# Second attention with position term and sink by TensorE products, input products in two sweeps, four probability buffers

## What is computed

```python
def second_block(x, p, w_in, w_pool, pool_scale, attn_sinks, w_out, ln1_g, ln1_b, ...):
    z = h @ w_in[i]                       # 1024 -> 512 (u_pool) + 512 (q) + 128 (k) + 128 (v)
    ...
    y_pool = pool_mixer(u_pool, w_pool[i], pool_scale[i])
    y_attn = sliding_window_attention(q, k, v, attn_sinks[i])
    mix = jnp.concatenate([y_pool, y_attn], axis=-1) @ w_out[i]
    h = layer_norm(DEEPNORM_ALPHA * h + mix, ln1_g[i], ln1_b[i])

def sliding_window_attention(q, k, v, sinks):   # 8 query heads, 2 key heads of 64, blocks of 128
    ...
    dist = (qi[:, None] + BLOCK - kj[None, :])
    bias = -slopes[:, :, None, None] * dist.astype(jnp.float32)[None, None]
    scores = jnp.where(mask[None, :, None, None], scores + bias[None, None], NEG_INF)
    m = jnp.maximum(jnp.max(scores, axis=-1, keepdims=True), sink)
    e = jnp.exp(scores - m)
    denom = jnp.sum(e, axis=-1, keepdims=True) + jnp.exp(sink - m)
    probs = (e / denom).astype(v.dtype)
```

## Time and profile before

| what | us |
|---|---|
| median of 3 runs (1540.32 to 1541.84) | 1541.45 |
| the profiled execution's own time | 1541.43 |
| its span in the profile | 1539.7 |
| TensorE busy | 1391.6 |
| VectorE busy | 503.3 |
| ScalarE busy | 310.0 |
| end of the input products to start of the `w_out_2` products | 48.4 |

### The profile page before, as it was taken

The page is one execution under the profiler, slowest core; times in us unless marked ns, Lnnn a source line. Parts: engine busy times, 40 slices in busy tenths (PEclk is TensorE's granted clock), DMA queues, the critical chain, the costliest instruction groups (busy, mean ns, idle before and its releaser), DMA issues.

```text
span 1539.7 us, 17201 instructions
## 1 busy us (share of the span) xinstructions
PE 1391.6 (90%) x6736; PEld 748.1 (49%) x6736; DVE 503.3 (33%) x913; ACT 310.0 (20%) x454; POOL 26.1 (2%) x41
## 2 busy tenths in 40 slices
PE   4998997989899899899899889999998878899998
PEld 2774455434334333334334334334333557699986
DVE  2646434213113113112112111121121454655565
ACT  3415232101101101101001001001011343544451
POOL 1000002000000000000000000000000200000000
PEclk9999997999999999999999999999999877999999
DMA  9208906899999999999999999999999630556540
GB/s 375 117 20 359 421 17 215 359 428 429 429 428 429 429 428 428 429 429 428 429 428 429 429 429 428 429 428 428 428 429 424 223 100 11 200 177 189 190 137 28
DMA packets 62680, 499.98 MB, mean 325 GB/s; under 512 B 6200, under 2 KB 22616, under 8 KB 34928
## 3 DMA queue, kind: packets, MB, share of 16 engines
q1 hardware_dynamic: 59472, 492.85, 77.7%
q0 software_dynamic: 1840, 5.82, 1.2%
q10 hardware_dynamic: 1328, 0.77, 0.2%
HBM read 498.37 MB, written 1.05 MB: 324 GB/s over the span
## 4 chain that ended last, share of the span: by engine, by line
PE 65%; DMA 22%; DVE 8%; issue 3%; ACT 1%; SPq 1%; DVEq 0%; ACTq 0%; PEldq 0%
PE bank L1447 28%; DMA ring<-in_w 20%; PE bank L586 17%; PE bank L624 15%; PE bank L644 2%; DMA ring<-in_w_ada 2%; DVE dk L699 1%; DVE mrows L703 1%; DVE dk L693 1%; PE bank L597 1%; PE bank L632 1%; PE bank L606 1%; DVE w_lo L446 1%; PE bank L1741 0%; PE bank L1629 0%
## 5 line engine op out<-in xcount | busy, mean ns | idle before, releaser
L586 PE MATMUL bank<-ring,xn 128*64 128x512 f32 x2048 | 468.0, 611 | 65.7 <-DMA ring<-in_w 64.1
L586 PEld LDWEIGHTS bank<-ring,xn 128*64 128x64 f32 x2048 | 163.5, 140 | 359.9 <-issue 359.9
L624 PE MATMUL bank<-ring,dq 128*64 128x512 f32 x1024 | 226.8, 595 | 0.0
L688 DVE TENSOR_SCALAR mrows<-bank 128x512 f32<-128x512 f32 x32 | 20.6, 686 | 477.7 <-PE bank L586 477.7
L658 ACT ACTIVATE sq<-mrows 128x512 f32<-128x512 f32 x32 | 19.6, 630 | 774.2 <-DVE mrows L688 774.2
L624 PEld LDWEIGHTS bank<-ring,dq 128*64 128x64 f32 x1024 | 70.6, 137 | 136.5 <-issue 133.8
L446 DVE TENSOR_TENSOR w_lo<-ring,w_hi 128x2048 fp32r<-128x2048 f32 (+1 forms) x41 | 89.7, 2194 | 42.4 <-ACT w_hi L439 42.4
L712 DVE TENSOR_TENSOR dk<-bank,bc 128x512 f32<-128x512 f32 x32 | 22.1, 692 | 236.2 <-PE bank L624 236.2
L439 ACT ACTIVATE w_hi<-ring 128x2048 fp32r<-128x2048 f32 (+1 forms) x44 | 78.5, 1791 | 38.0 <-PE bank L1447 26.6
L1447 PE MATMUL bank<-x_hi,w_hi 128*128 128x256 f32 x256 | 73.2, 286 | 1.8 <-DVE h_lo L1327 1.8
L1447 PE MATMUL bank<-x_hi,w_lo 128*128 128x256 f32 x256 | 73.1, 285 | 0.0
(11 more groups left out here) (358 smaller groups left out, 1464.2 us busy)
## 6 DMA issues: line engine op xcount, KB each, us to landing
ring<-in_w SPq DMA_DIRECT2D x192, 2048.0 KB, 17.1
ring<-in_w_ff SPq DMA_DIRECT2D x32, 1024.0 KB, 5.4
ring<-in_w_ada SPq DMA_DIRECT2D x24, 1024.0 KB, 16.5
ring<-in_w_out SPq DMA_DIRECT2D x8, 1024.0 KB, 8.3
ring<-in_w_in SPq DMA_DIRECT2D x8, 992.0 KB, 26.5
ring<-in_w_in SPq DMA_DIRECT2D x8, 640.0 KB, 11.4
ring<-in_w_ple_gate SPq DMA_DIRECT2D x4, 1024.0 KB, 4.8
xc<-in_ctx SPq DMA_DIRECT2D x1, 1024.0 KB, 5.0
```

Of the source, the lines that this page charges most:

```text
L586: m = pe.matmul(banks[bank_no][mine(i), :], gathered[:, k, mine(i)], rows_of(at + i, 2)[:, k % 2, q * 512:(q + 1) * 512], start=k == 0, st ...
L624: m = pe.matmul(banks[OUT_BANKS[c]][mine(i), :], actT[:, k, mine(i)], rows_of(8 + 2 * j + i, 4)[:, r, c * 512:(c + 1) * 512], start=k == 0 ...
L688: dve.tensor_scalar(gs[:, half * 512:half * 512 + 512], banks[GATE_BANKS[half]][:], LIMIT, None, ALU.min)\
```

## The change

1. **Input products in two sweeps.** First queries, keys and values for all eight chunks (768 columns), then `u` (512 columns) for all eight. Keys and queries are turned after the fourth chunk of the second sweep. The rounded parts of all eight chunks now lie side by side (`qkv_hi`, and the unused end of each ring slot), so that their rounding no longer waits for PE. Ring slots are given back in the second sweep.
2. **Position term by PE.** POOL builds once, during the first block, `slopes` (a diagonal matrix of the slope for each head) and `masks` (the negative distances). Each score sum starts with the fp32r product of the two.
3. **Sink as a column.** Column 0 of each score sum is the sink, added by a product of one row (`ones` x `sinks`). Maximum and sum of exponentials then contain it, and the five small DVE instructions and the small ACT exponential of each unit go. ACT takes the exponential straight from PSUM.
4. **Order.** `second_order`: score i, turn i-2, value i-3; `prob2` has four buffers; block 1 comes before block 0; the pool products stand among the units (after score 1 and score 3), the turn of the first half of the output after value 5, that of the second half among the `w_out_2` products. Block 1 has its keys from column 1 on, and values of the block behind without the first key (`v_behind`).
5. **Who does what.** DVE copies the turned probabilities instead of ACT. POOL makes the rest of two of the four `w_out_2` chunks (0 and 2), DVE that of 1 and 3. ACT loads its tables for the exponential and for the square root ahead.

```diff
-    for i in range(n_units + 2):
-        if i < n_units:
-            order.append(("score", i))
-        if 1 <= i <= n_units:
-            order.append(("turn", i - 1))
-        if i >= 2:
-            order.append(("value", i - 2))
+    for i in range(n_units + 3):
+        steps = [("score", i), ("turn", i - 2), ("value", i - 3)]
+        if i == 1:
+            steps.insert(1, ("pool", 0))
+        if i == 3:
+            steps.insert(1, ("pool_out", 0))
+        if i == 8:
+            steps.append(("half", 0))
...
+SPLIT_BY_POOL = list(range(AHEAD)) + [SPLIT.index(("w_out2", 0)), SPLIT.index(("w_out2", 2))]
...
+        prob2 = [dv[:, 2, :], dv[:, 3, :], dk[:, 2, :], dk[:, 3, :]]
...
(POOL, in the first block)
+            for h in range(QH):
+                step(pool.tensor_scalar(slopes[:, h, :].bitcast(F32R), ident[:], SLOPES[h], None, ALU.mult), "consts")
...
(ACT, score step)
-                        act.wait_ge(sem("masked"), u + 1)
-                        step(act.activation(prob2[:, u % 2, i * w:(i + 1) * w], prob2[:, u % 2, i * w:(i + 1) * w], ACT.Exp,
-                                            bias=soft[:, u, 4 + i:5 + i], accum_out=soft[:, u, 8 + i:9 + i]), wait=False)
-                    step(act.activation(soft[:, u, 10:12], soft[:, u, 6:8], ACT.Exp), "exp2_done")
+                        b = take(act, f"sw{u}_{i}")
+                        act.wait_ge(sem("max2_done"), 2 * u + i + 1)
+                        step(act.activation(prob2[u % 4][:, i * T:i * T + w], b[:, 0:w], ACT.Exp, bias=soft[:, u, 4 + i:5 + i],
+                                            accum_out=soft[:, u, 8 + i:9 + i]), tile=f"sw{u}_{i}")
...
(DVE, score and turn step)
-                        step(V.scalar_tensor_tensor(out=prob2[:, u % 2, i * w:(i + 1) * w], in0=neg_dist[:, 2 * P - w:2 * P],
-                                                    scalar=SLOPES[2 * h + i], in1=b[:, 0:w],
-                                                    op0=ALU.mult, op1=ALU.add), tile=f"sw{u}_{i}")
-                    step(V.tensor_reduce(soft[:, u, 0:2], prob2[:, u % 2, 0:2 * w].rearrange("p (i k) -> p i k", i=2),
-                                         AX, ALU.max))
-                    sink = sinks[:, 2 * h:2 * h + 2]
-                    step(V.tensor_tensor(soft[:, u, 2:4], soft[:, u, 0:2], sink, ALU.max))
-                    step(V.tensor_scalar(soft[:, u, 4:6], soft[:, u, 2:4], -1.0, None, ALU.mult), wait=False)
-                    step(V.tensor_tensor(soft[:, u, 6:8], sink, soft[:, u, 2:4], ALU.subtract), "masked")
+                        step(V.tensor_reduce(soft[:, u, 4 + i:5 + i], b[:, 0:w], AX, ALU.max, negate=True), "max2_done")
+                    if u == 5:
+                        rest_of_weights(dve, FIRST_OUT2 + 1)
+                elif what == "turn":
+                    b = take(dve, f"tw{u}")
+                    if u >= 2:
+                        dve.wait_ge(full(f"vw{u - 2}"), use(f"vw{u - 2}") + 1)
+                    step(V.tensor_copy(prob2T[u % 2][:, 0:2 * (blk + 1) * P], b[:, 0:2 * (blk + 1) * P]), tile=f"tw{u}")
...
(PE, score step)
+                    for i in range(2):
+                        mm(b[i][:, 0:masks[blk].shape[1]], slopes[:, 2 * h + i, :].bitcast(F32R), masks[blk][:].bitcast(F32R),
+                           True, False)
+                    for i in range(2):
+                        mm(b[i][:, 0:1], ones[0:1, :], sinks[0:1, 2 * h + i:2 * h + i + 1], False, False)
+                    for i in range(2):
+                        rows = slice(HD * i, HD * i + HD)
+                        mm(b[i][:, 1:w], q2T[rows, h, blk * P:(blk + 1) * P], k2T[rows, h // 2, blk:blk + w - 1], False, True)
```

More of the change, by code:

```diff
@@ L146 @@
 FRONT_TILES += [f"hfT0_{j}" for j in range(4)] + ["logits"] + [f"hfT1_{j}" for j in range(4)] + ["rank"]
[L148 to L154, removed]
+UNITS2 = [(h, b) for h in range(QH // 2) for b in reversed(range(NT))]
+BACK_TILES = [f"xT{t}_{j}" for t in range(NT) for j in range(2)] + [f"in{t}_{n}" for t in range(NT) for n in (1, 2)]
+BACK_TILES += ["in0_0", "in1_0", "kT", "qT0", "qT1"]
+for _what, _u in second_order(len(UNITS2)):
+    BACK_TILES += {"score": [f"sw{_u}_0", f"sw{_u}_1"], "turn": [f"tw{_u}"], "value": [f"vw{_u}"], "pool": ["pd0", "pd1"],
+                   "pool_out": ["py0", "py1"], "half": ["oT0"]}[_what]
+BACK_TILES += ["plT"] + [f"wo20_{n}" for n in range(2)] + ["oT1"] + [f"wo21_{n}" for n in range(2)]
 BACK_TILES += [f"ple{t}_{c}" for t in range(NT) for c in range(2)] + [f"h1T{t}_{j}" for t in range(NT) for j in range(2)]
@@ L966, in _ @@
                     act.wait_ge(moe("ring_freed", MAIN), freed_by(PAIRS - 1, 18 + AHEAD, MAIN))
-            for n in range(AHEAD, 8):
+            for n in range(AHEAD, FIRST_OUT2):
                 round_weights(act, n)
+            step(act.activation(stat[:, 57:58], stat[:, 56:57], ACT.Exp))
             for t in range(NT):
-                b = take(act, f"in{t}_0")
-                step(act.activation(u_tok[:, t, :], b[:], ACT.Copy), tile=f"in{t}_0")
                 b = take(act, f"in{t}_1")
@@ L1381, in _ @@
                          tile=f"vw{u}")
-            rest_of_weights(dve, 11)
-            for j in range(2):
-                rest_of(f"oT{j}", x_lo[:, 4 + 2 * j:6 + 2 * j, :], x_hi[:, 4 + 2 * j:6 + 2 * j, :])
+                elif what == "half":
+                    rest_of("oT0", x_lo[:, 4:6, :], x_hi[:, 4:6, :])
+            rest_of_weights(dve, FIRST_OUT2 + 3)
+            rest_of("oT1", x_lo[:, 6:8, :], x_hi[:, 6:8, :])
             def layer_norm(t, tiles, at, root, g, b_, done):
@@ new lines, in _ @@
+            bu = [claim(pe, f"in{t}_0") for t in range(NT)]
+            for k in range(KD):
+                if k == KD // 2:
+                    turn_keys_and_queries()
+                w = split_weights(pe, ("w_in2u", k))
+                for t in range(NT):
+                    m = mm3(bu[t][:], [v[:, k, t * P:(t + 1) * P].bitcast(F32R) for v in (x_hi, x_lo)], w,
+                            k == 0, k == KD - 1)
+                    if k == KD - 1:
+                        m.then_inc(full(f"in{t}_0"), 1)
@@ L1855, in _ @@
                         m.then_inc(full(f"wo20_{n}"), 1)
+            bw.update({(1, n): claim(pe, f"wo21_{n}") for n in range(2)})
             for n in range(2):
```

294 lines of the change are left out of this document (169 added, 125 removed).

## The result

| kernel | median (range) | ratio to before, 95% interval |
|---|---|---|
| before, run beside it | 1541.64 us (1540.32 to 1542.46, 4 runs) | |
| changed | 1529.23 us (1527.62 to 1532.94, 4 runs) | 0.9919 [0.9907, 0.993] |

The change saves 12.4 us, 0.8%. The time lies in the forecast range (1519 to 1534), but 4.7 us above the point, and it is the first rival that happened: the clock fell once, within the attention.

The account below looks back on a forecast made before the run. Bound: a DVE and ACT chain, between experts and `w_out_2` products, that also costs PE its clock. The path's terms end at 1291.8 against 1309.79, 18.0 us less, taken as 17 off 1541.43: 1524.5 us, range 1519 to 1534.

Parts of the forecast that it names:

- the first rival: Second attention: the clock falls once, from 1257 on; gain only 10 to 11 us, 1530.5 us; chance 0.25.
- Input products: Both sweeps: 28.98 us of products plus 1.50 of turns from 1210.60, ending at 1241.1, copies hidden.
- PE's score step: Position products, sinks and score pair on PE in the attention: 1.25 us (block 1) or 1.02 (block 0).
- signs of being wrong: Listed for the attention: PEclk 0.50, PE waiting for exponentials, overlong DVE or POOL rests, sinks over 0.25 us each.
- DVE's queue: From the pool outputs at 1250.5, DVE is the longest queue: 16.0 us, to 1266.5.
- My 1 us for hand-overs: Some ten more hand-overs between DVE, PE and ACT, about 0.1 us each: 1 us off the 18.0 gain.
- the full clock: Attention at 2.4 GHz throughout: the forecast itself, 1524.5 us, with its small slips (1519.5 to 1527); chance 0.55.
- the 1527 for a late fall: Variant within the attention: the clock falls only at 1264, costing 4 us, so 1527 us.
- 1.35 us of copies of keys and queries: Copies before the turns, 1.35 us in the path before, hidden by about 5.6 us of second-sweep products.
- POOL and DVE: Weight rests in the attention kept apart by 0.3 us; rival, POOL blocks DVE up to 4.6 us, up to 1529; chance 0.06.
- Half clock from the start of the stretch: PE at 1.2 GHz from the start becomes the bound; end 3.7 us later than before, 1545 us; chance 0.06.
- The change that doesn't reach the end: A `w_out_2` chunk or bank claim holds the products and the DVE gain vanishes: 1536 us; chance 0.08.

Follow-up runs that it names:

- `two_buf`: The changed kernel with two probability buffers instead of four; 1528.05 us, ratio to before 0.9909.
- `fillv1`: The changed kernel with one idle 256-column product on PE ahead of each value step's wait, from the second value on; 1525.02 us, ratio to before 0.9894.
- the repeat: The changed kernel run once more, unedited, as the base for the runs beside it; 1531.84 us, ratio to before 0.9929.
- `one_sweep`: The changed kernel with the input products in one sweep again, keys and queries turned behind all of them; 1533.41 us, ratio to before 0.9939.
- `dve_small`: The changed kernel with four small DVE instructions (128x2), results unused, added to each unit's maxima; 1536.12 us, ratio to before 0.9956.

## Why the prediction was right, and where it was not

**Input products: right.** The second sweep ended at 1240.06, 30.2 us after the first product; the sum had 30.5. Both hold some 2 to 3 us at half clock at the start, which the sum took over unseen with the 28.98 of before; where the clock was back earlier, it is 29.0 (`two_buf`). DVE's copies for keys began at 1227.00 and were done by 1229.3, four us before the turns.

**PE's score step: mis-sized.** Neighbouring starts in PE's timeline of the changed kernel:

```profile
1240.06 0.40 PE L1485 MATMUL bank<-mask,slopes 128*128 128x256 f32 x2
1240.39 0.60 PE L1485 MATMUL bank<-kr,ones 1*128 1x1 f32 x4
1240.92 0.70 PE L1485 MATMUL bank<-sq,xn 64*128 64x255 f32 x4
1241.55 0.44 PE L1485 MATMUL bank<-mask,slopes 128*128 128x130 f32 x2
1241.92 0.60 PE L1485 MATMUL bank<-kr,ones 1*128 1x1 f32 x4
```

Two position products take 0.33 to 0.41 us in these steps (0.24 in the sum), and 0.51 behind `pd`, four sink records 0.53 (0.44), the score pair 0.63 (0.58). A step of block 1 measured at 1252.49 is 1.57 us instead of 1.25, the one of block 0 at 1241.55 is 1.32 instead of 1.02. Four of them stand ahead of the pool outputs, 1.2 us. That is about the whole delay of DVE's start: 41.05 us into the stretch instead of 39.9. A sink is 0.265 us; over 0.25 was one of the prediction's signs of being wrong.

**DVE's queue: right.** In `fillv1`, where the clock doesn't interfere, it runs from 1251.10 to 1267.26, 16.2 us (sum: 16.0), with the rest of chunk 1 at 2.29 us in the middle, and then waits 1.06 for ACT's rounding of `oT0`, as the sum had it. The `w_out_2` products begin 60.3 us into the stretch there, against 58.9 forecast. Of these 1.4 us 0.85 lie ahead of DVE's start, the other 0.5 are in its queue (0.2), in the wait (0.15) and behind it (0.2). My 1 us for hand-overs roughly covers them, but most of what it covers are products priced too low, which is luck.

**The clock: the wrong choice.** I gave the full clock 0.55 and one fall 0.25, on the ground that no hole as empty as before's (0.26 us of work in 2.5) was left. The fall needed no such hole. It came after stretches with PE busy 2.22 and 1.99 us of 2.50 and a single hole of 0.79 us. The rival's mechanism is the one that happened. Its time of the products, 1274.0 (measured 1273.94) after a fall at 1257 (measured 1257.0), is closer than its terms: it had the fall at 4.5 us, against `fillv1` it is 3.8 (64.1 - 60.3 us into the stretch), and the score steps that it lacked and a stretch that began 0.8 us earlier made up the rest. It was also 2.4 us too dear where it had the first products at half clock: the clock came back at 1270.6, before them. In the repeat it came back late, and 1.0 us of that cost showed. Its gain of 10 to 11 us leaves out, as the 1527 for a late fall does, the 1 us for hand-overs that the forecast takes off. The rival's 1530.5 stands between the first median, 1529.23, and the repeat's, 1531.84.

**Sweeps: undersized in the argument.** I counted 1.35 us of copies of keys and queries that the second sweep hides, and nothing for ACT's copies of the turned tiles. `one_sweep` lost 3.6 to 5.5 us: its hole is those copies of ACT's, 1.29 us, and behind it the clock falls under the pool products. The 1.35 us itself is in no run of the changed kernel.

**POOL and DVE: right, by a narrow margin.** DVE's rest of chunk 1 ran from 1258.83 to 1261.1, POOL's second from 1261.56; 0.4 us apart where I had 0.3. What a meeting costs, `dve_small` shows: a DVE instruction that began inside POOL's waited to its end (2.2 us and more), while POOL's, beginning 0.35 us before the end of DVE's, took 0.2 us longer. The full 4.6 us of the prediction no run shows. The first POOL rest, beside the first scores and pool outputs, met instructions with a PSUM operand only.

**The rivals that didn't happen.** Half clock from the start of the stretch (1545) is ruled out by PEclk 1.00 up to 1255. `one_sweep` shows how near it was: one hole of 1.29 us brought the clock down at 1242.6, though only for 7 us. The change that doesn't reach the end (1536) is ruled out by the 248.8 us behind the stretch.

**The number.** The range of 1519 to 1534 held because it took in the fall of the clock, to which I had given less than half the chance of the full clock. The full-clock forecast, 1524.5, is what `fillv1` measures (1525.02), where the fall is prevented.

## What to carry to other kernels

When an edit takes work off the engine that bounds a stretch, ask whether the engine that becomes next is TensorE: from that point on its clock, free until then, is in the sum, and the same idle product that was worth nothing before (0.9996) is worth 4 to 6 us. Price the holes as well as the work: an idle product of 0.4 us ahead of a wait of 0.8 us holds the clock here, but it must stand before the fall, and a second one in each place cost 1.4 us. When you compare lengths inside profiles, look at the clock at the start of the length too. And when GpSimd gets large instructions, look through VectorE's queue for small ones that read only SBUF: one that begins inside a GpSimd instruction can wait to its end, 2.4 to 2.6 us here.

## What was unexpected of the hardware

- The clock fell to 1.2 GHz with PE busy for 4.2 of 5.0 us (1252.5 to 1257.5), and stayed there for 13.6 us in one run and about 20 in another of the same kernel, with PE busy for all of each 2.5 us from 1257.5 to 1270. In `fillv1` a later stretch with 1.87 us of work in 2.5 (1267.5 to 1270, a hole of 0.63 us) brought no fall, nor did a hole of 0.91 us before 1272.84 in the changed kernel itself, just behind the clock's return. Neither the busy share nor the length of one hole alone tells which will.
- A VectorE instruction on 128x2 floats took 2.35 to 2.58 us instead of 0.16 or 0.17 when it began inside a GpSimd instruction of 4.5 us, with one SBUF operand as with two. RECIPROCAL on as much, from SBUF, kept its 0.17 us inside such an instruction.
- A product with one row of weights and one column, four records of which add a sink to two score sums, takes 0.13 us a record (0.53 for four, at 2.4 GHz). That is more than a record of a turn with 128 columns (0.44 for four): one column saves nothing. At 1.2 GHz it is 0.235 (0.94 for four), so it isn't a fixed time either.
